# All expert weights in 8 KB runs, two ring slots a step, and fewer unread products between the down steps

## The chip, the cores and the metric

The kernel runs on one core of a Trainium2 chip. The metric is the device time of one execution in microseconds (us), lower is better; three runs of the kernel before gave 1293.96, 1295.03 and 1295.28, median 1295.03. The core has five engines that work side by side and meet at semaphores: TensorE (PE, matrix products; its weight loads are listed as PEld), VectorE (DVE), ScalarE (ACT), GpSimd (POOL) and SyncE (SP, which here only issues DMA transfers). 16 DMA engines move data between HBM and the on-chip memory SBUF, whose rows are its 128 partitions. TensorE writes to eight PSUM banks.

## The reference

256 tokens of width 1024 (float32) pass a first block, a state-space mixer and a mixture of experts, and then four mixer layers. The change touches only the mixture of experts, cut here to what is computed:

```python
def hierarchical_moe(hn, w_router_group, w_router_expert, w_gate, w_up, w_down):
    # 4 groups of 8 experts; each token goes to the 2 best experts of its best group
    ...
    def run_block(args):          # xb: tokens of one expert e
        xb, e = args
        return (jax.nn.silu(xb @ w_gate[e]) * (xb @ w_up[e])) @ w_down[e]
    ...
    out = jnp.zeros((n, d), jnp.float32).at[row_token].add(ys.astype(jnp.float32) * row_gate[:, None])
```

`w_gate` and `w_up` are 32 x 1024 x 512 and `w_down` is 32 x 512 x 1024, all float32: 6 MiB an expert, 192 MiB (201.3 MB) in all. Every expert's weights are read once in each execution.

## The kernel before, in words

The program is a chain of stages: the state-space mixer (`ssd`), the router and the mixture of experts (`moe`), and the layers `fox0`, `gla`, `gdn` and `fox1`. Large weights arrive through a ring of four slots of 2 MiB (`ring`, `SLOTS` = 4), filled by SP. A slot is filled by two DMAs of 1 MiB, one for each half; both raise the semaphore `ready[i]` of the slot.

**The expert stage.** Experts are taken four at a time (`QUAD`), in `NQ` = 8 groups. A group has 12 steps (`MOE_STEPS`), each of which uses one slot: eight for the products with gate and up (`STEPS_UP`), in turn gate and up, then four for down. An up step holds, for four experts, 256 rows of the weight matrix: partition p takes rows 2p and 2p+1 of each expert, which lie side by side in HBM, 2 x 512 x 4 bytes = 4 KB (`up_v`, L437, `r=2`). A down step holds 128 rows of 1024 columns, again 4 KB for each partition and expert (`down_v`, L438). So every slot is loaded in runs of 4 KB (`moe_loads`, L456).

TensorE (`pe_quad`, L2530) waits for the slot of a step, multiplies (8 matmuls, each of which the trace counts as 2 instructions: 16 a step; the four experts share the array side by side, 32 columns each), and raises `ring_used`, on which SP waits before it fills a slot again (L551 in the loop over the groups 2 to 7). Between the up and the down steps TensorE gathers the tokens of the next group (`gather`, L2525), transposes the hidden rows (L2553), and waits for ScalarE's copy of them. After the down steps it scatters the result (L2574). Since partition p holds rows 2p and 2p+1, the gathered tokens are picked with stride 2 (`own` in `gather`), and their norm gains `g_ffn` are laid out to match.

`unread(n, b)` (L2138) issues n small bf16 products into a bank whose result nobody reads. `pe_quad` issues 16 of them before each of the last three down steps.

**The first two groups** are loaded early. Besides the four ring slots they use five further buffers (`extra`, L447) in memory that the stage does not need: group 0 has steps 0 to 3 and 9 to 11 in the ring and 4 to 8 in the extra buffers. So nine steps can be loaded before TensorE has used one; step 9 is the first that waits for `ring_used` (`put`, L504, with `released`).

**After the stage** SP loads the first block of `fox0` behind the last down weights (L509); the other blocks wait for `moe_done`. ScalarE and DVE split each weight block into a high and a low part (L673, L1202).

## Time and profile before

| | |
|---|---|
| median of 3 runs | 1295.03 us (1293.96 to 1295.28) |
| profiled execution, its own time | 1292.94 us |
| its span (first to last instruction) | 1291.2 us |
| TensorE clock granted, mean | 0.964 of full |
| PE / DVE / ACT busy | 86% / 50% / 34% |
| HBM read | 312.52 MB |

The span is cut by the page into 40 slices of 32.3 us. One digit is the share of a slice in which an engine was busy, in tenths; the line GB/s is what the DMA engines moved. The difference of 1.74 us between the time and the span lies around the span, and 2.09 us separate the profiled execution from the median. A granted clock of 1.00 is TensorE's level of 2.4 GHz, 0.50 its level of 1.2 GHz.

### The profile page before, as it was taken

What the parts mean: (1) busy time and instruction counts of PE and PEld (TensorE: products, weight loads), DVE (VectorE), ACT (ScalarE), POOL (GpSimd) and SP (SyncE); (2) the same over time, 40 slices, a digit from 0 to 9 for tenths busy, and PEclk for the clock granted to TensorE, in tenths of its full rate; (3) what the DMA queues carried; (4) which work ended last, traced back from release to release, by engine and by line L of the source; (5) the groups of instructions that cost most, each with busy time, mean ns of one, the idle gap of its engine ahead of it and who ended that gap; (6) DMA issues with size and microseconds to landing.
All of it is one profiled execution on the core that took longest, in us unless ns stands there. A gap on an engine that the chain in (4) does not pass through costs nothing.

```text
span 1291.2 us, 19652 instructions
## 1 busy us (share of the span) xinstructions
PE 1106.5 (86%) x8060; PEld 811.6 (63%) x8060; DVE 644.5 (50%) x1265; ACT 439.2 (34%) x691; POOL 8.0 (1%) x35
## 2 busy tenths in 40 slices
PE   8999899897676758585858999999999979899998
PEld 7999767543131314131414789887779869778897
DVE  6787578420101111020104767667567965656685
ACT  5554435100000000000003556536346653255563
POOL 1000000000000000000000000000000000000000
PEclk9999999999898989898989999999999989899999
DMA  8575345999999999999998974254324530056600
GB/s 299 144 260 196 131 157 196 398 409 409 409 409 410 409 410 410 410 409 410 410 410 296 289 223 155 106 196 143 118 94 168 183 79 4 1 130 172 235 19 33
DMA packets 120005, 314.66 MB, mean 244 GB/s; under 512 B 17139, under 2 KB 17386, under 8 KB 119674
## 3 DMA queue, kind: packets, MB, share of 16 engines
q1 hardware_dynamic: 116864, 310.78, 65.9%
q0 software_dynamic: 352, 2.11, 0.4%
q8 instruction: 54, 0.88, 0.3%
q10 hardware_dynamic: 2714, 0.71, 0.3%
q14 instruction: 21, 0.17, 0.0%
HBM read 312.52 MB, written 1.06 MB: 243 GB/s over the span
## 4 chain that ended last, share of the span: by engine, by line
PE 58%; DMA 28%; DVE 8%; ACT 3%; issue 2%; SPq 1%; DVEq 0%; ACTq 0%
DMA ring<-in_w_up 18%; DMA ring<-in_w_down 10%; PE bank L2250 7%; PE bank L2243 7%; PE bank L2247 7%; PE bank L2225 6%; PE bank L2229 6%; PE bank L2232 6%; PE bank L2540 3%; PE bank L2563 2%; DVE w_l L1202 1%; PE bank L2158 1%; DMA ring<-in_w_in 1%; PE bank L2646 1%; ACT w_h L673 1%
## 5 line engine op out<-in xcount | busy, mean ns | idle before, releaser
L1202 DVE TENSOR_TENSOR w_l<-ring,w_h 128x1024 fp32r<-128x1024 f32 x204 | 246.6, 1221 | 90.7 <-ACT w_h L673 89.0
L673 ACT ACTIVATE w_h<-ring 128x1024 fp32r<-128x1024 f32 x204 | 213.6, 1056 | 176.4 <-PE bank L2232 88.7
L2540 PE MATMUL bank<-ring,cm 128*32 128x512 f32 x880 | 137.1, 754 | 101.0 <-DMA ring<-in_w_gate 61.5
L2540 PEld LDWEIGHTS bank<-ring,cm 128*32 128x32 f32 x880 | 27.7, 124 | 208.6 <-issue 78.5
L2243 PE MATMUL bank<-w_h,hnT_h 128*128 128x512 f32 x480 | 135.6, 405 | 5.1 <-DVE cm L1829 1.9
L2250 PE MATMUL bank<-w_l,hnT_h 128*128 128x512 f32 x480 | 129.7, 392 | 5.5 <-DVE w_l L1202 5.5
L2247 PE MATMUL bank<-w_h,hnT_l 128*128 128x512 f32 x480 | 129.7, 392 | 0.0
L1676 DVE SCALAR_TENSOR_TENSOR cm<-cm,bank 128x512 f32<-128x512 f32 x8 | 5.5, 688 | 215.0 <-ACT cm L895 215.0
L2250 PEld LDWEIGHTS bank<-w_l,hnT_h 128*128 128x128 f32 x480 | 89.6, 188 | 27.4 <-DVE w_l L1202 8.5
L2247 PEld LDWEIGHTS bank<-w_h,hnT_l 128*128 128x128 f32 x480 | 90.6, 189 | 20.0 <-DVE hnT_l L1317 0.2
L2243 PEld LDWEIGHTS bank<-w_h,hnT_h 128*128 128x128 f32 x480 | 86.9, 190 | 25.2 <-issue 4.5
L895 ACT ACTIVATE cm<-bank 128x512 f32<-128x512 f32 x8 | 4.8, 597 | 266.1 <-PE bank L2540 266.1
L2225 PE MATMUL bank<-hnT_h,w_h 128*128 128x256 f32 x576 | 84.1, 289 | 0.0
L2229 PE MATMUL bank<-hnT_l,w_h 128*128 128x256 f32 x576 | 80.9, 283 | 0.0
L2232 PE MATMUL bank<-hnT_h,w_l 128*128 128x256 f32 x576 | 80.8, 283 | 0.0
L2225 PEld LDWEIGHTS bank<-hnT_h,w_h 128*128 128x128 f32 x576 | 74.9, 191 | 2.0 <-issue 1.2
L2563 PE MATMUL bank<-ring,cm 128*32 128x512 f32 x496 | 59.6, 598 | 18.7 <-DMA ring<-in_w_down 13.8
L2232 PEld LDWEIGHTS bank<-hnT_h,w_l 128*128 128x128 f32 x576 | 74.3, 192 | 0.0
L2229 PEld LDWEIGHTS bank<-hnT_l,w_h 128*128 128x128 f32 x576 | 74.3, 192 | 0.0
L1686 DVE COPY cm<-bank 128x512 f32<-128x512 f32 x8 | 5.5, 691 | 124.6 <-PE bank L2563 124.6
L2141 PEld LDWEIGHTS bank<-ident 128*128 128x128 bf16 x446 | 43.4, 102 | 28.0 <-issue 20.1
L2141 PE MATMUL bank<-ident 128*128 128x256 bf16 x446 | 57.1, 285 | 1.6 <-POOLq L587 1.6
(442 smaller groups left out, 1354.9 us busy)
## 6 DMA issues: line engine op xcount, KB each, us to landing
ring<-in_w_down SPq DMA_DIRECT2D x62, 1024.0 KB, 15.9
ring<-in_w_gate SPq DMA_DIRECT2D x56, 1024.0 KB, 15.6
ring<-in_w_up SPq DMA_DIRECT2D x54, 1024.0 KB, 15.8
ring<-in_fox_w_in SPq DMA_DIRECT2D x32, 1024.0 KB, 11.3
ring<-in_w_in SPq DMA_DIRECT2D x22, 1024.0 KB, 9.6
ring<-in_gla_w_in SPq DMA_DIRECT2D x12, 1024.0 KB, 6.3
ring<-in_gdn_w_in SPq DMA_DIRECT2D x12, 1024.0 KB, 6.8
ring<-in_w_out SPq DMA_DIRECT2D x8, 1024.0 KB, 6.3
```

Source lines behind the costliest of these rows:

```text
L673: af(part(w_h, u, width), w, ACT.Copy).then_inc(s["high_ready"], 1)
L1202: v.tensor_tensor(part(w_l, u, width), w, part(w_h, u, width).bitcast(F32), ALU.subtract).then_inc(s["low_ready"], 1)
L2141: mm(bank[b][:, 0:2 * P], ident[:].bitcast(BF16)[:, 0:P], ident[:].bitcast(BF16), start=True, stop=True)
L2158: x = mm(out_rows, w[:, k, c], x_part[:, k, :], start=(w is sw_h and x_part is hnT_h and k == 0), stop=(w is sw_l and k == KD - 1))
L2225: mm(dst, wh[:, k, :], xh[:, k, :], start=(k == 0), stop=False)
L2229: mm(dst, wh[:, k, :], xl[:, k, :], start=False, stop=False)
L2232: x = mm(dst, wl[:, k, :], xh[:, k, :], start=False, stop=(k == KD - 1))
L2243: mm(dst, hnT_h[:, k, tt], wh[:, j, :], start=(first and k == ends[0]), stop=False)
L2247: mm(dst, hnT_l[:, k, tt], wh[:, j, :], start=False, stop=False)
L2250: x = mm(dst, hnT_h[:, k, tt], wl[:, j, :], start=False, stop=(last and k == ends[1]))
L2540: x = mm(bank[a][CAP * e:CAP * (e + 1), :], m_xg[:, 2 * b + r, CAP * e:CAP * (e + 1)], expert_of(w, e)[:, r * FF:(r + 1) * FF], start=(b = ...
L2563: x = mm(bank[3 + n][CAP * e:CAP * (e + 1), :], m_ht[:, c * P + CAP * e:c * P + CAP * (e + 1)], expert_of(w, e)[:, n * BLK:(n + 1) * BLK], ...
```

## The change

**Layout.** `up_v` now takes four adjacent rows for a partition (`r=4`) and `down_v` two, so that a run is 8 KB. One DMA of 1 MiB then holds one expert's rows instead of two experts', and a slot holds two experts instead of four. A matrix product of all four experts needs two slots, so TensorE's loop takes steps in pairs: it waits for both slots, does 16 matmuls (32 instructions), and releases the first slot with the last matmul of expert 1 and the second with that of expert 3. Gate and up alternate by pairs. Tokens and gains are picked with stride 4, the hidden rows with stride 2.

**The last group** is written out behind the loop, on SP and on TensorE. Its last two down steps keep the old form: 4 KB runs, one slot each (`last_v`, `last_loads`, `by_chunk`).

**Unread products.** 24 stand between the two down pairs in place of 16 before each of three steps; group 0 has none; the last group has 24 and then 16 before its two single steps. In a group of the loop that is 24 instead of 48.

**Waits.** ScalarE's tanh of the gate bank waits for 6 released slots instead of 7. The code for tokens beyond an expert's capacity (`ov_slot`) takes two ring slots a step as well; it does not run with these inputs.

```diff
+        g_ffn = sb("g_ffn", [P, 2, KD // 2])
         cols = sb("cols", [16, 8])
...
-        up_v = [w.rearrange("(q j) (b p r) f -> q b p j (r f)", j=QUAD, p=P, r=2) for w in (w_gate, w_up)]
-        down_v = w_down.rearrange("(q j) (c p) n -> q c p j n", j=QUAD, p=P)
+        up_v = [w.rearrange("(q j) (b p r) f -> q b p j (r f)", j=QUAD, p=P, r=4) for w in (w_gate, w_up)]
+        down_v = w_down.rearrange("(q j) (c p r) n -> q c p j (r n)", j=QUAD, p=P, r=2)
+        last_v = w_down.rearrange("(q j) (c p) n -> q c p j n", j=QUAD, p=P)
...
         def moe_loads(halves, q, j):
 
             if j < STEPS_UP:
-                return [(halves[h].rearrange("p (e x) -> p e x", e=QUAD // 2),
-                         up_v[j % 2][q, j // 2][:, 2 * h:2 * h + 2, :]) for h in (0, 1)]
-            return [(halves[h].rearrange("p (e f) -> p e f", e=QUAD // 2),
-                     down_v[q, j - STEPS_UP][:, 2 * h:2 * h + 2, :]) for h in (0, 1)]
+                v, first = up_v[(j // 2) % 2][q, j // 4], 2 * (j % 2)
+            else:
+                v, first = down_v[q, (j - STEPS_UP) // 2], 2 * (j % 2)
+            return [(halves[h], v[:, first + h, :]) for h in (0, 1)]
+
+        def last_loads(halves, q, c):
+
+            return [(halves[h].rearrange("p (e f) -> p e f", e=QUAD // 2), last_v[q, c][:, 2 * h:2 * h + 2, :]) for h in (0, 1)]
...
-                    (g_ffn[:], norm_ffn[0].rearrange("(b p r) -> p b r", p=P, r=2))) + tuple(
+                    (g_ffn[:], norm_ffn[0].rearrange("(b p r) -> p b r", p=P, r=4))) + tuple(
...
-                    with sp.Fori(2, NQ) as q:
+                    with sp.Fori(2, NQ - 1) as q:
                         for j in range(MOE_STEPS):
                             i = (n + j) % SLOTS
                             sp.wait_ge(s["ring_used"], q * MOE_STEPS + (j - SLOTS + 1))
                             sp.sem_inc(s["sp_turn"], 1)
                             for dst, src in moe_loads(ring_halves(i), q, j):
                                 sp.dma_start(dst, src).then_inc(ready[i], 16)
+                    q = NQ - 1
+                    for j in range(MOE_STEPS):
+                        i = (n + j) % SLOTS
+                        sp.wait_ge(s["ring_used"], q * MOE_STEPS + (j - SLOTS + 1))
+                        sp.sem_inc(s["sp_turn"], 1)
+                        for dst, src in (moe_loads(ring_halves(i), q, j) if j < MOE_STEPS - 2 else last_loads(ring_halves(i), q, j - STEPS_UP)):
+                            sp.dma_start(dst, src).then_inc(ready[i], 16)
 
...
 
             def act_quad(it, used, base):
-                act.wait_ge(used, base + STEPS_UP - 1)
+                act.wait_ge(used, base + STEPS_UP - 2)
...
                 pe.wait_ge(s["moe_acc"], acc)
                 for k in ks:
                     for t in range(NT):
-                        own = slice(2 * P * (k // 2) + k % 2, 2 * P * (k // 2 + 1), 2)
+                        own = slice(4 * P * (k // 4) + k % 4, 4 * P * (k // 4 + 1), 4)
                         x = mm(b4(5 + k // 4)[:, k % 4, :], hn[:, t, own], m_S[:, t, :],
                                start=(t == 0), stop=(t == NT - 1))
                     if k % 4 == 3:
...
 
-            def pe_quad(q, it, g, wait_slot, release, second_half=None):
+            def pe_quad(q, it, g, wait_slot, release, second_half=None, by_chunk=False):
                 pe.wait_ge(s["moe_h"], it + 1)
-                for j in range(STEPS_UP):
+                for j in range(0, STEPS_UP, 2):
                     if j == STEPS_UP // 2 and second_half is not None:
                         gather(0, 1, second_half)
                     if j % (STEPS_UP // 2) == 0:
                         pe.wait_ge(s["moe_xg"], g * 2 + (1 + 2 * j // STEPS_UP))
-                    w, a, b = wait_slot(q, j), j % 2, j // 2
-                    for r in (0, 1):
+                    w, a, b = wait_slot(q, j) + wait_slot(q, j + 1), (j // 2) % 2, j // 4
+                    for r in range(4):
                         for e in range(QUAD):
-                            x = mm(bank[a][CAP * e:CAP * (e + 1), :], m_xg[:, 2 * b + r, CAP * e:CAP * (e + 1)], expert_of(w, e)[:, r * FF:(r + 1) * FF],
-                                   start=(b == 0 and r == 0), stop=(b == KD // 2 - 1 and r == 1), tile_position=(0, CAP * e))
-                    x.then_inc(release, 1)
+                            x = mm(bank[a][CAP * e:CAP * (e + 1), :], m_xg[:, 4 * b + r, CAP * e:CAP * (e + 1)], w[e][:, r * FF:(r + 1) * FF],
+                                   start=(b == 0 and r == 0), stop=(b == 1 and r == 3), tile_position=(0, CAP * e))
+                            if r == 3 and e % 2:
+                                x.then_inc(release, 1)
                 gather(g + 1, it + 1)
...
                 for c in range(STEPS_DOWN):
-                    x = tr(b4(2)[:, c, :], m_h[:, c * P:(c + 1) * P], ident[:])
+                    own = slice(2 * P * (c // 2) + c % 2, 2 * P * (c // 2 + 1), 2)
+                    if by_chunk and c >= 2:
+                        own = slice(c * P, (c + 1) * P)
+                    x = tr(b4(2)[:, c, :], m_h[:, own], ident[:])
                 x.then_inc(s["moe_ht"], 1)
                 pe.wait_ge(s["moe_htc"], it + 2)
                 pe.wait_ge(s["moe_acc"], it + 1)
-                for c in range(STEPS_DOWN):
-                    if c:
-                        unread(16, 2)
+
+                def down(c, n, e, w):
+
+                    return mm(bank[3 + n][CAP * e:CAP * (e + 1), :], m_ht[:, c * P + CAP * e:c * P + CAP * (e + 1)], w,
+                              start=(c == 0), stop=(c == STEPS_DOWN - 1), tile_position=(0, CAP * e))
+
+                for c2 in range(1 if by_chunk else 2):
+                    if c2 and second_half is None:
+                        unread(24, 2)
+                    w = wait_slot(q, STEPS_UP + 2 * c2) + wait_slot(q, STEPS_UP + 2 * c2 + 1)
+                    for r in (0, 1):
+                        for n in (0, 1):
+                            for e in range(QUAD):
+                                x = down(2 * c2 + r, n, e, w[e][:, r * D + n * BLK:r * D + (n + 1) * BLK])
+                                if r and n and e % 2:
+                                    x.then_inc(release, 1)
+                for c in (2, 3) if by_chunk else ():
+                    unread(24 if c == 2 else 16, 2)
                     w = wait_slot(q, STEPS_UP + c)
                     for n in (0, 1):
                         for e in range(QUAD):
-                            x = mm(bank[3 + n][CAP * e:CAP * (e + 1), :], m_ht[:, c * P + CAP * e:c * P + CAP * (e + 1)],
-                                   expert_of(w, e)[:, n * BLK:(n + 1) * BLK], start=(c == 0), stop=(c == STEPS_DOWN - 1),
-                                   tile_position=(0, CAP * e))
+                            x = down(c, n, e, expert_of(w, e)[:, n * BLK:(n + 1) * BLK])
                     x.then_inc(release, 1)
 
...
-            with pe.Fori(2, NQ) as q:
+            with pe.Fori(2, NQ - 1) as q:
                 pe_quad(q, q, q, ring_slot, s["ring_used"])
+            pe_quad(NQ - 1, NQ - 1, NQ - 1, ring_slot, s["ring_used"], None, True)
```

The three places at which the order of instructions matters, word for word. A line has the source line, the operation, the bank written and the tile read, and in brackets the semaphores that it waits for; `ring` is the slot ring, `slot_ready0` to `3` its semaphores, x7 seven of the same. Line numbers shift by 13 or more in the changed file.

TensorE at the start of group 0, before:

```order
L2540 MATMUL bank0<-ring,cm 32x512 [waits slot_ready3,moe_xg,moe_h]
L2540 MATMUL bank0<-ring,cm 32x512 x7
L2540 MATMUL bank1<-ring,cm 32x512 [waits slot_ready0]
L2540 MATMUL bank1<-ring,cm 32x512 x7
L2540 MATMUL bank0<-ring,cm 32x512 [waits slot_ready1]
L2540 MATMUL bank0<-ring,cm 32x512 x7
L2540 MATMUL bank1<-ring,cm 32x512 [waits slot_ready2]
L2540 MATMUL bank1<-ring,cm 32x512 x7
L2525 MATMUL bank6<-cm,hn 128x128 [waits moe_acc,moe_sel]
```

TensorE at the same place, now:

```order
L2553 MATMUL bank0<-ring,cm 32x512 [waits slot_ready3,slot_ready0,moe_xg,moe_h]
L2553 MATMUL bank0<-ring,cm 32x512 x15
L2553 MATMUL bank1<-ring,cm 32x512 [waits slot_ready2,slot_ready1]
L2553 MATMUL bank1<-ring,cm 32x512 x15
L2538 MATMUL bank6<-cm,hn 128x128 [waits moe_acc,moe_sel]
```

The four steps of 8 matmuls have become two of 16, and each waits for two slots; the first release stands at the 14th matmul of a step instead of the 8th.

TensorE at the end of a group, before (the loop's last down steps):

```order
L2563 MATMUL bank3<-ring,cm 32x512 [waits slot_ready2]
L2563 MATMUL bank3<-ring,cm 32x512 x3
L2563 MATMUL bank4<-ring,cm 32x512 x4
L2141 MATMUL bank2<-ident 128x256 x16
L2563 MATMUL bank3<-ring,cm 32x512 [waits slot_ready3]
L2563 MATMUL bank3<-ring,cm 32x512 x3
L2563 MATMUL bank4<-ring,cm 32x512 x4
L2141 MATMUL bank2<-ident 128x256 x16
L2588 REGISTER_ALU
L2563 MATMUL bank3<-ring,cm 32x512 [waits slot_ready0]
```

TensorE at the end of the last group, now:

```order
L2577 MATMUL bank3<-ring,cm 32x512 [waits slot_ready1,slot_ready2,moe_acc,moe_htc]
L2577 MATMUL bank3<-ring,cm 32x512 x3
L2577 MATMUL bank4<-ring,cm 32x512 x4
L2577 MATMUL bank3<-ring,cm 32x512 x4
L2577 MATMUL bank4<-ring,cm 32x512 x4
L2154 MATMUL bank2<-ident 128x256 x24
L2577 MATMUL bank3<-ring,cm 32x512 [waits slot_ready3]
L2577 MATMUL bank3<-ring,cm 32x512 x3
L2577 MATMUL bank4<-ring,cm 32x512 x4
L2154 MATMUL bank2<-ident 128x256 x16
L2577 MATMUL bank3<-ring,cm 32x512 [waits slot_ready0]
```

The first two down steps have become one pair; the last two stand as they were, with 24 and 16 unread products (L2141, now L2154) ahead of them.

SP's last loads of the stage, before (inside the loop):

```order
L553 DMA ring<-in_w_down 128x2x1024 [waits ring_used]
L553 DMA ring<-in_w_down 128x2x1024
L550 REGISTER_ALU
L547 REGISTER_ALU
L547 COMPARE_AND_BRANCH
```

SP at the same place, now (behind the loop):

```order
L565 DMA ring<-in_w_down 128x2048 [waits ring_used]
L565 DMA ring<-in_w_down 128x2048
L565 DMA ring<-in_w_down 128x2x1024 [waits ring_used]
L565 DMA ring<-in_w_down 128x2x1024
L565 DMA ring<-in_w_down 128x2x1024 [waits ring_used]
L565 DMA ring<-in_w_down 128x2x1024
```

A half of a slot was 128 partitions x 2 runs of 1024 elements (4 KB); it is now one run of 2048 elements (8 KB), except in the last two steps. SP's order of loads and waits is otherwise the same.

## Rows read from the trace of the kernel before

**Rows 1.** The page, section 2: DMA busy tenths and GB/s by slice.
```profile
DMA  8575345999999999999998974254324530056600
GB/s 299 144 260 196 131 157 196 398 409 409 409 409 410 409 410 410 410 409 410 410 410 296 289 223 155 106 196 143 118 94 168 183 79 4 1 130 172 235 19 33
```

**Rows 2.** The chain that ended last, by line, window 400 to 500 us.
```profile
by line: DMA ring<-in_w_up 71.4%; DMA ring<-in_w_down 35.7%; PE bank L2540 7.9%; SPq L553 2.2%; PE bank L2563 2.0%; issue 1.0%; SPq L551 0.1%
```

**Rows 3.** Timeline of PE, one group: start, us, what, idle time before and its cause.
```profile
464.00 3.62 PE L2540 MATMUL bank<-ring,cm 128*32 128x512 f32 x16 [3.21 <-DMA ring<-in_w_gate]
...
489.59 1.92 PE L2540 MATMUL bank<-ring,cm 128*32 128x512 f32 x16 [1.49 <-DMA ring<-in_w_up]
491.45 4.04 PE L2525 MATMUL bank<-cm,hn 128*128 128x128 f32 x32
...
496.82 1.92 PE L2563 MATMUL bank<-ring,cm 128*32 128x512 f32 x16 [0.69 <-ACT cm L899]
498.68 1.92 PE L2141 MATMUL bank<-ident 128*128 128x256 bf16 x16
500.53 1.92 PE L2563 MATMUL bank<-ring,cm 128*32 128x512 f32 x16
```

**Rows 4.** DMA queues in one group, 423 to 484.44 us: packets, MB, share of 16 engines.
```profile
DMA packets 6528, 25.17 MB, mean 410 GB/s; under 512 B 384, under 2 KB 384, under 8 KB 6528
q1 hardware_dynamic: 6528, 25.17, 102.6%
```

**Rows 5.** The software queue at 747 to 754 us, then at 1192 to 1199 us.
```profile
q0 software_dynamic: 144, 1.05, 36.0%
q0 software_dynamic: 144, 1.05, 35.8%
```

**Rows 6.** Timeline of SP around the first release of a slot.
```profile
223.66 0.88 SPq L509 DMA_DIRECT2D ring<-in_w_up  x2
...
228.11 3.06 SPq L543 DMA_DIRECT2D spare<-in_w_down  x2
244.58 4.63 SPq L509 DMA_DIRECT2D ring<-in_w_down  x6
```

**Rows 7.** Timeline of PE, first two products of group 0.
```profile
242.60 7.07 PE L2540 MATMUL bank<-ring,cm 128*32 128x512 f32 x64 [0.90 <-issue]
249.61 2.15 PE L2525 MATMUL bank<-cm,hn 128*128 128x128 f32 x16
```

**Rows 8.** Windows: us, busy by engine, PEclk, DMA share, GB/s; two restarts, one slow step.
```profile
223.00:224.00 1.00, 1.00 (x10) 0.96 (x9) 1.00 (x2) 0.32 (x1) 0.00 (x0) 1.00 0.00 0
224.00:225.00 1.00, 1.00 (x6) 0.83 (x5) 1.00 (x3) 0.52 (x2) 0.00 (x0) 1.00 0.56 66
...
244.00:246.00 2.00, 2.00 (x24) 0.68 (x19) 0.00 (x0) 0.00 (x0) 0.00 (x0) 1.00 1.17 389
246.00:248.00 2.00, 2.00 (x24) 0.79 (x20) 0.00 (x0) 0.00 (x0) 0.00 (x0) 1.00 0.88 309
248.00:250.00 2.00, 2.00 (x19) 0.71 (x12) 0.00 (x0) 0.00 (x0) 0.00 (x0) 1.00 0.96 373
...
474.40:477.70 3.30, 3.30 (x16) 0.58 (x16) 0.00 (x0) 0.00 (x0) 0.00 (x0) 0.50 1.03 412
```

**Rows 9.** Timeline of PE, end of the last group, and ACT behind it.
```profile
691.14 1.92 PE L2141 MATMUL bank<-ident 128*128 128x256 bf16 x16
694.42 1.92 PE L2563 MATMUL bank<-ring,cm 128*32 128x512 f32 x16 [1.36 <-DMA ring<-in_w_down]
697.34 3.70 PE L2574 MATMUL bank<-cm 128*128 128x512 f32 x8 [1.00 <-DVE cm L1686]
...
699.93 2.95 ACT L673 ACTIVATE w_h<-ring 128x1024 fp32r<-128x1024 f32 x3 [2.92 <-DMA ring<-in_fox_w_in]
```

**Rows 10.** DMA queues at 967 to 970 us, where runs are 2 KB.
```profile
DMA packets 612, 1.22 MB, mean 407 GB/s; under 512 B 16, under 2 KB 16, under 8 KB 612
q1 hardware_dynamic: 612, 1.22, 104.6%
```

**Rows 11.** Windows in which 4 KB runs moved more than 410 GB/s.
```profile
230.00:235.00 5.00, 4.73 (x30) 3.95 (x31) 4.41 (x22) 0.00 (x0) 0.00 (x0) 0.70 1.03 420
250.00:252.00 2.00, 1.76 (x15) 1.56 (x14) 0.20 (x1) 0.00 (x0) 0.00 (x0) 1.00 1.03 420
```

More of the change, by code:

```diff
@@ L246, in build @@
         w_gup = sb("w_gup", [16, BLK])
-        g_ffn = sb("g_ffn", [P, KD // 2, 2])
+        g_ffn = sb("g_ffn", [P, 2, KD // 2])
         cols = sb("cols", [16, 8])
@@ L560, in _ @@
                             with sp.Fori(0, NQ) as q:
-                                for j in range(MOE_STEPS):
-                                    for dst, src in moe_loads(ring_halves(0), q, j):
-                                        sp.dma_start(dst, src).then_inc(ov_ready, 16)
-                                    sp.wait_ge(ov_used, (p - 1) * (NQ * MOE_STEPS) + q * MOE_STEPS + (j + 1))
+                                for j in range(0, MOE_STEPS, 2):
+                                    for i in (0, 1):
+                                        for dst, src in moe_loads(ring_halves(i), q, j + i):
+                                            sp.dma_start(dst, src).then_inc(ov_ready, 16)
+                                    sp.wait_ge(ov_used, (p - 1) * (NQ * MOE_STEPS) + q * MOE_STEPS + (j + 2))
                                     sp.sem_inc(s["sp_turn"], 1)
@@ L2602, in ov_slot @@
                     def ov_slot(q, j):
-                        pe.wait_ge(ov_ready, (p - 1) * (32 * NQ * MOE_STEPS) + q * (32 * MOE_STEPS) + 32 * (j + 1))
-                        return ring_halves(0)
+                        pe.wait_ge(ov_ready, (p - 1) * (32 * NQ * MOE_STEPS) + q * (32 * MOE_STEPS) + 64 * (j // 2 + 1))
+                        return ring_halves(j % 2)
                     with pe.Fori(0, NQ) as q:
```

## The prediction

> **What bounds the kernel now.** I read the slices first. From the eighth to the twenty-first the DMA engines move 398 to 410 GB/s without a break, while TensorE is between 50% and 90% busy [rows 1]. That is the expert stage. The chain that ended last says the same: in 100 us of it nearly all is loads of up and down weights (its pieces overlap, so the shares pass 100%) [rows 2]. The timeline of one group shows TensorE at each step waiting for its slot, 1.5 or 3.2 us, and then working 1.9 or 3.6 us [rows 3]. A group of 12 slots (25.17 MB) takes 61.44 us and repeats to the hundredth. So the end of the stage is set by bytes over rate, counted from where the stream last had to wait for TensorE. Work on TensorE inside a group is free so long as slots come back in time.
>
> **The longer runs.** In one group every DMA engine carries 6144 / 16 = 384 packets of 4 KB (and 24 of under 512 B), so one packet every 61.44 / 384 = 160.0 ns. The packets were busy for 102.6% of 16 x 61.44 us = 1008.6 us, or 164 ns each: each overlaps the next by 4 ns [rows 4]. The trace has packets of 8 KB too, 128 in each of two transfers of the software queue: 36.0% of 16 x 7 us is 40.3 us, 315 ns each, and 35.8% gives 313 [rows 5]. That is 14 ns below two packets of 4 KB (328). With the same overlap of 4 ns an 8 KB packet comes every 310 ns. A slot is 256 such packets, 16 an engine: 4.96 us instead of 5.12, 0.16 us less. If the overlap grows with the packet, 310 becomes 160 x 314/164 = 306 (0.22 us a slot); if runs make no difference to a full stream, it is 320 (nothing). I take 310, the value nearest to the rows of 8 KB themselves.
>
> A page of the Trainium skill speaks against this size of gain: DMA: Bandwidth & Descriptors, section "Why small descriptors are slow (HBM only)", gives a packet about 3 cycles beside one for each 32 bytes, and calls concatenation worth it only up to 256 B. By that, an estimate: 8 KB needs 259 cycles instead of 262, 1.1% of 85 x 5.12 us or 5.0 us, and the whole change would bring 2.8 us (1292.2 us). The rows of 4 and 8 KB show a larger step (14 of 328 ns, 4%), so the trace does not agree with that size; it is weighed as a rival below.
>
> **How many slots gain.** There are 96 slots. The nine of the four ring slots and five further buffers (steps 0 to 8 of group 0) don't wait for TensorE's releases, and the stream then stops for TensorE: SP ended issuing at 231.17 and issued step 9 at 244.58 [rows 6]. What the first nine save is therefore lost at this wait. 87 remain, two of them in 4 KB runs: 85 x 0.16 = 13.6 us saved.
>
> **The first release comes later.** TensorE starts group 0 at 242.60 and needs 7.07 us for four steps, 1.77 each [rows 7]. Before, the first slot was released after one step, by 244.52, and SP issued at 244.58 [rows 6]. By then the stream had nearly run dry: the three windows from 244 to 250 us move 389, 309 and 373 GB/s instead of 410, which is 0.8 us of transfer [rows 8]. Now both slots come back after two steps, 242.60 + 3.6 = 246.2, so step 9 is issued 1.7 us later. An issue into an empty queue brings its first bytes about 1 us later (issued 223.66, none before 224, 66 GB/s in the next microsecond) [rows 6, 8]. The restart is bound by the issue before and after, so the cost is the shift, 1.7 us; if the ramp from fully empty costs another 0.8 us, 2.5. The second pair is released by 250, when 4 MiB (9.9 us) are queued again, so there is no second stop.
>
> **Pairs in the steady groups.** The ring holds two pairs. A pair landed must be released before the next has landed, less 1 us until an issue brings bytes: within 9.92 - 1 = 8.9 us. An up pair takes 3.6 us at the high clock. At the low clock (granted 0.50, 1.2 GHz [rows 8]) a step took 3.62 us, after 3.2 us of idling; the next step had the high clock again [rows 3]. Idling before a pair grows to some 6 us, so I expect each up pair to lose one such stretch: 3.6 + 1.7 = 5.3 us. That fits. After the last up pair come the gather, transposes and copies, 5.4 us from 491.45 to 496.82 [rows 3]; 5.3 + 5.4 = 10.7 us, 0.8 us after the first down pair has landed. It is released at 0.8 + 3.6 = 4.4 us: fits. After it 24 unread products take 2.8 us (16 take 1.86, 498.68 to 500.53 [rows 3]), ready before the second down pair. So these pairs cost nothing; what hides them is the stream, and the price once it fails is in the fourth rival.
>
> **The end.** The last single step runs 1.92 us after the last slot landed, then the scatter follows [rows 9]. This piece is as before. But TensorE must be there: from the start of the last group's down pair it needs 3.6 + 2.8 + 1.9 + 1.9 = 10.2 us, and the last slot lands 10.24 us after that pair. It starts the pair 0.8 us late at 5.3 us an up pair, on time at 3.6, 2.7 us late at 7.2. I take 0.5 us, bounds 0 and 2.7. The first block of the next layer is now issued after the down pair, about 6 us ahead of the last landing, so it still queues directly behind it; ScalarE waits for this block until 699.93 as it does now [rows 9], and all later stages shift as a whole.
>
> **At nothing.** Fewer unread products, and none in group 0: TensorE idles there for loads or runs ahead of them. Stride 4 in the gather: 4.04 us at stride 2; twice that would still be within the 8.9 us. The gains `g_ffn` are half as many small packets. The last group written out: straight code in place of one pass of a loop. ScalarE's tanh keeps a full up pair ahead of its use.
>
> **Sum.** 13.6 - 1.7 - 0.5 = 11.4 us off the profiled execution's 1292.94 (its span of 1291.2 and 1.74 around it): 1281.5. The median of the runs lies 2.09 us higher, so the forecast is **1283.6 us**. By the bounds: at 306 ns 85 x 0.22 = 18.7 less 1.7 gives 1278.0; at 310 with 2.5 and 2.7 lost, 1286.6. The forecast's own range is 1279 to 1288.
>
> **Rivals.**
> *Second, a part of the rate* (9%). In a full stream of 2 KB runs a packet comes every 16 x 3 / (612 - 16) us = 80.5 ns, though busy for 1.046 of that, 84 ns [rows 10]. From 2 to 4 KB the stream thus gained 1 ns in 161, while busy time gained 4 ns in 168. If most of the 14 ns is hidden in the same way and 315 ns are reached, 0.08 us a slot remain: 6.8 - 2.2 = 4.6 us, 1290.4 us. The page's estimate of 1292.2 belongs here.
>
> *Third, no gain in rate* (12%). 2 KB runs stream at 407 GB/s and 4 KB runs at 410 [rows 4, 10]: this looks like a limit that run length doesn't touch. The SP queue may also cut a run of 8 KB in two, as all 8 KB packets seen were the software queue's. Against it: 4 KB runs have moved 420 GB/s for 5 us and for 2 us [rows 11], so memory and ports carry more. Then only the two costs stand: 1295.03 + 2.2 = 1297.2 us, up to 1299.
>
> *Fourth, slower: pairs starve the ring* (7%). If TensorE stays at the low clock through the last up pair and the gather, it takes 7.2 + 8.1 + 2.0 = 17.3 us, the down pair starts 7.4 us late and is released 11.0 us after landing, 2.1 past the 8.9. It decides from a release later than 8.9 us on. Seven groups at 2.1 are 15 us, and the end comes 7.4 us late: 13.6 - 1.7 - 15 - 7.4 = -10.5, 1305.5 us. Against it: in all groups the clock was back after one slow step, and stood at full in the gather [rows 3].
>
> **How the numbers follow.** Forecast 72%, the rivals 9, 12 and 7%. No change means within 0.2%, 2.6 us, about what can be told for this kernel. Faster: the forecast and nearly all of the second, 80%. Same: the third, but for its upper end, and what is left of the second, 11%. Slower: the fourth and the end of the third, 9%. The range starts at 1279.5 and reaches over the second rival to 1293; the third and the fourth lie outside.
>
> **What would show it.** The steady groups: 61.44 us should become 59.5 (12 x 4.96), the stream 410 become 423 GB/s, and packets number half. If the group stays at 61.4, the third rival holds; if the stream drops below its rate once in a group, beside the first down pair, the fourth. The first release should bring SP's issue at 246.2 to 246.5 and a window under 200 GB/s near 246. The last down step should start about 11 us earlier than 694.42, at 683, with little or no idling ahead of it, and the stages behind it should keep their lengths. The forecast is wrong if the group takes over 60.3 us or the later stages change by more than a microsecond.

## The result, and the profile after

The changed kernel takes 1302.21 us (median of 5, 1300.99 to 1307.34), the kernel before 1295.03 us: ratio 1.0062, 95% interval 1.0044 to 1.0081. The forecast was 1283.6 us. The change makes the kernel slower, by 7 to 8 us, and the time lies outside the range given. In other comparisons below the kernel before had medians of 1295 to 1298 us, so only ratios are compared.

The page of the changed kernel, slices and packets, answers [rows 1]:

```profile
PEclk9999999898888878797979999999999989999999
DMA  8575345899999999999997974353325530045600
GB/s 298 140 262 195 130 164 196 363 422 420 398 395 424 399 423 397 423 400 422 400 422 252 290 228 140 121 195 130 130 69 185 173 94 3 2 128 168 231 25 33
DMA packets 95687, 314.70 MB, mean 242 GB/s; under 512 B 16883, under 2 KB 17130, under 8 KB 71290
```

The stream now alternates between slices at 420 GB/s or more and slices at about 400, where every slice was 409 or 410. The rate is there, and something takes it away again. One group of 61.3 us, 409.5 to 470.83 us, as in [rows 4]:

```profile
GB/s 411 422 417 422 422 411 427 422 427 411 427 427 427 422 427 422 427 411 411 427 411 427 422 417 427 144 198 427 417 427 427 427 427 427 427 427 427 417 427 422
q1 hardware_dynamic: 3454, 25.15, 99.0%
```

Each slice is 1.53 us. 38 of the 40 run at 411 to 427 GB/s, two at 144 and 198: there is one stop a group. TensorE's timeline around it (start, duration, idle time before), which answers [rows 3]:

```profile
429.38 6.20 PE L2553 MATMUL bank<-ring,cm 128*32 128x512 f32 x32 [3.84 <-DMA ring<-in_w_up]
435.51 7.73 PE L2538 MATMUL bank<-cm,hn 128*128 128x128 f32 x32
...
444.63 3.64 PE L2577 MATMUL bank<-ring,cm 128*32 128x512 f32 x32 [0.69 <-ACT cm L912]
448.20 2.79 PE L2154 MATMUL bank<-ident 128*128 128x256 bf16 x24
```

The last up pair takes 6.20 us and the gather 7.73, in place of 4.04. So the first down pair, which landed some 9.9 us after 429.38, isn't started before 444.63 nor released before 448.2. SP's issues (SPq is SP's queue; x8 are four slots in two halves each), and the stream there (windows: length, PE busy, granted clock, DMA share, GB/s):

```profile
425.68 11.91 SPq L558 DMA_DIRECT2D ring<-in_w_down  x8
448.50 2.19 SPq L558 DMA_DIRECT2D ring<-in_w_gate  x4
```
```profile
430.00:434.00 4.00, 4.00 (x24) 0.50 1.00 418
436.00:442.00 6.00, 6.00 (x28) 1.00 1.01 422
448.00:449.00 1.00, 1.00 (x12) 1.00 0.30 123
449.00:450.00 1.00, 1.00 (x12) 1.00 0.68 90
450.00:451.00 1.00, 1.00 (x14) 1.00 0.69 262
451.00:452.00 1.00, 1.00 (x12) 1.00 1.03 434
```

In the three windows from 448 us 475 of 3 x 422 = 1266 are moved, a loss of 791 / 422 = 1.9 us. A group of 12 slots at 4.96 us is 59.5 us, and 59.5 + 1.9 = 61.4, the old period.

There are six such stops, near 325, 387, 449, 511, 571 and 633 us. At the first two the last up pair had taken only 5.34 us. The second, with TensorE, SP and the stream:

```profile
368.86 5.34 PE L2553 MATMUL bank<-ring,cm 128*32 128x512 f32 x32 [4.51 <-DMA ring<-in_w_up]
...
383.24 3.64 PE L2577 MATMUL bank<-ring,cm 128*32 128x512 f32 x32 [0.69 <-ACT cm L912]
```
```profile
387.12 2.17 SPq L558 DMA_DIRECT2D ring<-in_w_gate  x4
```
```profile
386.00:387.00 1.00, 1.00 (x14) 1.00 0.73 303
387.00:388.00 1.00, 1.00 (x11) 1.00 0.14 57
388.00:389.00 1.00, 1.00 (x11) 1.00 1.04 164
389.00:390.00 1.00, 1.00 (x11) 1.00 0.79 336
```

The loss is again 828 / 422 = 2.0 us, and this group takes 61.42 us (399.64 - 338.22). The two ends of the stage, as in [rows 6, 7, 9]:

```profile
248.66 4.33 SPq L514 DMA_DIRECT2D ring<-in_w_down  x6
```
```profile
240.10 4.00 PE L2538 MATMUL bank<-cm,hn 128*128 128x128 f32 x16 [0.70 <-DVE cm L1664]
245.00 7.07 PE L2553 MATMUL bank<-ring,cm 128*32 128x512 f32 x64 [0.90 <-issue]
...
676.41 5.34 PE L2553 MATMUL bank<-ring,cm 128*32 128x512 f32 x32 [4.60 <-DMA ring<-in_w_up]
...
690.77 3.64 PE L2577 MATMUL bank<-ring,cm 128*32 128x512 f32 x32 [0.69 <-ACT cm L912]
...
700.78 1.92 PE L2577 MATMUL bank<-ring,cm 128*32 128x512 f32 x16
703.72 3.67 PE L2604 MATMUL bank<-cm 128*128 128x512 f32 x8 [1.02 <-DVE cm L1699]
```

Step 9 is issued at 248.66 in place of 244.58 (+4.1 us), and the scatter starts at 703.72 in place of 697.34 (+6.4). A low-clock stretch in a later stage adds most of another 1.7 us; the span is 1299.3 us, 8.1 longer. At its start (both kernels wait 2.2 us for VectorE before it, but the old one's four products take 1.20 us):

```profile
898.30 1.68 PE L2263 MATMUL bank<-w_l,hnT_h 128*128 128x512 f32 x4 [2.22 <-DVE w_l L1215]
899.77 1.91 PE L2256 MATMUL bank<-w_h,hnT_h 128*128 128x512 f32 x4
```

### The profile page after: what moved, and what is told of

The parts are those of the page before. It is cut to its first block, busy times and chain, and to the rows that moved or that the text cites. A ratio compares the mean times of both kernels' runs of the same rounds, so it can differ in the third digit from the quotient of the medians.

```text
span 1299.3 us, 19222 instructions
## 1 busy us (share of the span) xinstructions
PE 1122.6 (86%) x7860; PEld 839.6 (65%) x7860; DVE 644.7 (50%) x1265; ACT 439.6 (34%) x691; POOL 8.1 (1%) x35
## 4 chain that ended last, share of the span: by engine, by line
PE 70%; DMA 16%; DVE 8%; ACT 3%; issue 2%; SPq 1%; ACTq 0%; DVEq 0%
DMA ring<-in_w_up 15%; PE bank L2263 7%; PE bank L2256 7%; PE bank L2553 7%; PE bank L2260 7%; PE bank L2242 6%; PE bank L2238 6%; PE bank L2245 6%; PE bank L2538 5%; PE bank L2577 4%; PE bank L2154 2%; DVE w_l L1215 1%; SPq L558 1%; PE bank L2171 1%; DMA ring<-in_w_in 1%
## 5 line engine op out<-in xcount | busy, mean ns | idle before, releaser
L2553 PE MATMUL bank<-ring,cm 128*32 128x512 f32 x880 | 144.7, 809 | 103.5 <-DMA ring<-in_w_up 66.7
L2553 PEld LDWEIGHTS bank<-ring,cm 128*32 128x32 f32 x880 | 37.3, 142 | 209.2 <-issue 150.1
L2538 PEld LDWEIGHTS bank<-cm,hn 128*128 128x128 f32 x288 | 68.0, 329 | 8.6 <-issue 7.8
L2538 PE MATMUL bank<-cm,hn 128*128 128x128 f32 x288 | 69.9, 402 | 0.7 <-DVE cm L1664 0.7
L2577 PE MATMUL bank<-ring,cm 128*32 128x512 f32 x496 | 58.2, 595 | 4.8 <-ACT cm L912 4.8
```

The source lines that it names most:

```text
L2538: x = mm(b4(5 + k // 4)[:, k % 4, :], hn[:, t, own], m_S[:, t, :], start=(t == 0), stop=(t == NT - 1))
L2553: x = mm(bank[a][CAP * e:CAP * (e + 1), :], m_xg[:, 4 * b + r, CAP * e:CAP * (e + 1)], w[e][:, r * FF:(r + 1) * FF], start=(b == 0 and r = ...
L2577: return mm(bank[3 + n][CAP * e:CAP * (e + 1), :], m_ht[:, c * P + CAP * e:c * P + CAP * (e + 1)], w, start=(c == 0), stop=(c == STEPS_DOW ...
```

## The experiments

Twelve kernels were run, in four comparisons with the kernel before. The table keeps start and stream apart: when step 9 is issued, how long it is from there to the transposes behind the stage ("stage"; 701.98 - 244.58 = 457.4 us in the kernel before), and the stream over 270 to 670 us, all from profiled executions. Between the scatter and these transposes run 5 waits 1.1 us longer than the others and run 8 0.5 us longer, outside the stream; where that matters the scatter is used instead.

| kernel | step 9 | stage | GB/s | ratio, 95% interval |
|---|---|---|---|---|
| before | 244.58 | 457.4 | 409 | |
| changed | 248.66 | 459.7 | 410 | 1.0062 [1.0044, 1.0081] |
| 1 changed, packed gather | 247.51 | 453.2 | 413 | 0.9969 [0.9939, 0.9999] |
| 2 before, stride 4 | 247.25 | 458.3 | 409 | 1.0038 [1.0013, 1.0063] |
| 3 changed, 4 KB runs | 250.23 | 467.6 | 403 | 1.0115 [1.0081, 1.0148] |
| 4 before, packed gather | 244.72 | 457.5 | 409 | 0.9989 [0.9966, 1.0012] |
| 5 = 1 + 40 unread products | 246.88 | 446.9 | 421 | 0.9964 [0.9942, 0.9986] |
| 6 changed + 40 unread | 250.66 | 449.5 | 419 | 0.9984 [0.9963, 1.0005] |
| 7 = 5 + halved first pair | 245.41 | 446.0 | 421 | 0.9941 [0.9922, 0.9961] |
| 8 = 5 in 4 KB runs | 252.12 | 459.8 | 409 | 1.0054 [1.0032, 1.0076] |
| 9 = 7, 8 KB to the end | 248.54 | 448.3 | 421 | 0.9955 [0.9938, 0.9971] |
| 10 = 7 with 24 unread | 249.52 | 445.9 | 421 | 0.9952 [0.9926, 0.9977] |
| 11 = 7 without unread | 245.19 | 454.6 | 413 | 0.9959 [0.9934, 0.9983] |
| 12 = 7 with 32 unread | 245.70 | 446.6 | 421 | 0.9928 [0.9900, 0.9956] |

**1. The gather without a stride.** VectorE writes the normalised tokens already in the order in which the gather reads them.

```
-  v.tensor_scalar(hn[:, t, :], x_res[:, t, :], ...
+  v.tensor_scalar(hn[:, t, :].rearrange("p (b r j) -> p b r j", r=4, j=P),
+                  x_res[:, t, :].rearrange("p (b j r) -> p b r j", r=4, j=P), ...
-  own = slice(4 * P * (k // 4) + k % 4, 4 * P * (k // 4 + 1), 4)
+  own = slice(P * k, P * (k + 1))
```

> The changed kernel, but the normalized tokens are stored permuted (VectorE writes them so), and the gather reads its 128 columns side by side. Theory S (the stride of 4 doubles the gather, 7.73 us instead of 4.04, and that lets the stream of weights stop once in each group): gather at most 4.0 us, no stop, 59.5 us a group, last scatter about 18 us earlier than in the changed kernel (703.7), median about 1284 us. Rival P (working in pairs of slots is itself too coarse for a ring of four slots): gather shorter, but the stop in each group stays, median over 1296. Rival C (the low clock of TensorE in the up pairs, with fewer unread products): up pairs still take 6 us and a stop of about 1 us a group remains, median about 1291.

The gather takes 3.84 us, and the ratio falls from 1.0062 to 0.9969, 12 us, give or take 5; by the trace the scatter comes 7.6 us earlier (696.08 for 703.72). The stride was most of what was wrong. But 1284 us and a scatter 18 us earlier were expected, and the stream makes only 413 GB/s: up pairs are still slow, and some dips remain. That is rival C (1291 us) and not theory S alone (timeline and two windows of this kernel):

```profile
425.68 6.26 PE L2554 MATMUL bank<-ring,cm 128*32 128x512 f32 x32 [3.77 <-DMA ring<-in_w_up]
431.88 3.84 PE L2539 MATMUL bank<-cm,hn 128*128 128x128 f32 x32
...
437.10 3.64 PE L2578 MATMUL bank<-ring,cm 128*32 128x512 f32 x32 [0.69 <-ACT cm L912]
```
```profile
434.00:435.00 1.00, 1.00 (x12) 1.00 1.02 270
435.00:436.00 1.00, 1.00 (x11) 1.00 0.72 303
```

**2. The stride alone, in the kernel before.** The gather reads every fourth column instead of every second; it gathers other columns, so only the time counts.

```
-  own = slice(2 * P * (k // 2) + k % 2, 2 * P * (k // 2 + 1), 2)
+  own = slice(4 * P * (k // 4) + k % 4, 4 * P * (k // 4 + 1), 4)
```

> The kernel before, with the gather reading tokens with stride 4 instead of 2 (it gathers other columns than the weights in the slots belong to: only the time counts). Theory S: gather 7.7 us in each group; with one slot a step the ring absorbs it (the first down step starts 3.7 us later, its slot is due 15 us after that), so the groups stay at 61.44 us; only the first release (2 us) and the end of the last group (about 2 us) are later: median about 1299. Rival P: the stride costs little by itself, under 1 us: 1295 to 1296.

The gather takes 7.73 us, the groups keep 61.44 us (from 404.62 to 466.06), step 9 comes 2.7 us later and the stage is 0.9 us longer. With single slots, back in time, the stride costs only the start and the tail: 3.6 us by the trace, 5 us (2 to 8) in the median, where 4 were expected.

**3. The changed kernel in runs of 4 KB**, with its pairs and strides. A slot holds half the run of all four experts.

```
-  return [(halves[h], v[:, first + h, :]) for h in (0, 1)]
+  own = slice((j % 2) * (SLOT // QUAD), (j % 2 + 1) * (SLOT // QUAD))
+  return [(halves[h]..., v[:, 2 * h:2 * h + 2, own]) for h in (0, 1)]
```

> The changed kernel with the same pairs, strides and unread products, but every slot loaded in 4 KB runs (a slot holds half of the run of all four experts). Theory S: a slot takes 5.12 us again and the stream does not stop, since the down pair is released 18.9 us after the last up pair landed and the deadline moves from 18.8 to 19.5 us; 61.44 us a group, the same as with 8 KB, so a median within 3 us of the changed kernel, 1300 to 1305. If instead the faster stream still gives most of its gain, this is 8 us or more slower than the changed kernel, 1310.

The stage is 8 us longer than the changed kernel's and the stream at 403 GB/s, under the old 409. So the changed kernel had kept a part of its faster stream. The guess of 1300 to 1305 us was a miss: stops cost the slower stream too. The ratio of 1.0115 stands for 1310 us, the other value named.

**4. The packed gather in the kernel before**, by the edit of run 1 with r=2.

> The kernel before, with the tokens stored permuted so that the gather reads side by side instead of with stride 2. Theory S: the weight load of the gather falls from 196 ns to about 120 to 190 ns, the gather from 4.04 us to 3.9 or less; groups stay at 61.44, the start of group 0 moves by less than 0.5 us either way (VectorE's permuted write may cost 0.7 us): no change within 1 us of 1295.

No change, 0.9989. Packing by itself brings nothing there, so what it brought in run 1 is the cure of the stride.

**5. The clock of the up pairs.** In `pe_quad`, ahead of the waits for the second to fourth up pair:

```
+  if j and second_half is None:
+      unread(40, 2)
```

> The kernel with the packed gather, and 40 unread products (about 4.65 us at 24 in 2.79) ahead of the waits for the second, third and fourth up pair of every group but the first. Theory C (what is left after the packed gather is the low clock: TensorE idles 6.3 us before an up pair, then works at 1.2 GHz for 6.0 to 6.2 us of the pair, so that the first down pair is released too late once a group): the up pairs take 3.64 us, the dip to about 300 GB/s beside the first down pair goes, a group takes 59.5 us in place of 60.9 to 61.4, seven groups bring 6 to 9 us, and the time comes to 1283 to 1287, ratio 0.991 to 0.993 against the kernel before. Rival M (the memory or the queue gives no more than 413 GB/s over a group, and the dips are its own): the pairs get short, the group stays at 60.9 or more, the time stays at 1291 to 1293 (0.997).

The dips are gone, the up pairs of the steady groups take 3.64 us, and a group takes 59.7 us (first gate pairs at 394.88 and 454.58 us). Timeline, and two windows of 60 us:

```profile
404.74 3.64 PE L2556 MATMUL bank<-ring,cm 128*32 128x512 f32 x32 [1.74 <-DMA ring<-in_w_up]
...
414.77 3.64 PE L2556 MATMUL bank<-ring,cm 128*32 128x512 f32 x32 [1.92 <-DMA ring<-in_w_gate]
```
```profile
300.00:360.00 60.00, 46.42 (x387) 1.00 1.01 421
420.00:480.00 60.00, 46.45 (x387) 1.00 1.01 422
```

By the trace the stage is 6.3 us shorter than in run 1, and 7.4 us if it is taken to the scatter (441.2 for 448.6). The median doesn't show it: 0.9964 after 0.9969, from different comparisons, where 0.991 to 0.993 were expected. In the profiled execution the stages behind the transposes took 595.8 us, in that of the kernel before 589.2: see "Later stages" and runs 11 and 12.

**6. The same products with the stride left in.**

> The changed kernel (gather with stride 4, 7.7 us) with the same 40 unread products ahead of the up pairs. By the deadline sum: from the landing of the last up pair 3.64 + 7.73 + about 1.3 (transposes, copies) = 12.7 us until TensorE starts the first down pair, 2.8 after its landing; released at 6.4 us, within 8.9. So if stride and low clock only matter through the sum of both, this kernel streams at 59.5 us a group as well and lands within 2 to 3 us of the kernel with both cures (1286 to 1289: group 0 still starts 1.2 us later and its gather is 2 us longer). Rival: the slow gather costs by itself (weight loads from the same memory as the landing packets, or a chain ScalarE and VectorE that hangs on it), then the group stays above 60.5 and the time near 1296 to 1300.

From 420 us on the stream makes 422 GB/s with the gather of 7.73 us still there; TensorE releases the first down pair 6.4 us after its landing. So the stride fits as long as the pairs are quick: it needs the low clock beside it to stop the groups, while the low clock alone still costs some (run 1). What the stride costs by itself is the start (step 9 at 250.66, where the clock was low as well), a stop before 360 us (408 GB/s from 300 to 360) and a small one behind it (419 from 360 to 420).

```profile
430.52 3.64 PE L2555 MATMUL bank<-ring,cm 128*32 128x512 f32 x32 [1.75 <-DMA ring<-in_w_up]
434.10 7.73 PE L2538 MATMUL bank<-cm,hn 128*128 128x128 f32 x32
...
443.21 3.64 PE L2579 MATMUL bank<-ring,cm 128*32 128x512 f32 x32 [0.69 <-ACT cm L912]
```
```profile
420.00:480.00 60.00, 50.04 (x382) 1.00 1.01 422
```

**7. An early first release.** Steps 0 and 1 of group 0 in half runs of all four experts, released one after the other:

```
+  if j < 2 and isinstance(q, int) and q == 0:     # in moe_loads: 4 KB runs, as in run 3
-  if r == 3 and e % 2:
+  if (r % 2 and e == 3) if halved else (r == 3 and e % 2):
       x.then_inc(release, 1)
```

> The kernel with the packed gather and the 40 unread products, and also the first gate pair of group 0 in runs of 4 KB that hold half a run of all four experts, so that its first slot is released after one step (8 products a half, 1.8 us) as in the kernel before. If the start is as the prediction took it (the shift of the first release is lost one for one), step 9 is issued 1.7 us earlier, and the end comes 1.7 us earlier than in the kernel without it: 1282 to 1285, ratio about 0.990. Rival: the stream restarts from a deeper empty queue or stops a second time for the next pair, the gain is then under 0.8 us.

Step 9 is issued 2.0 us after TensorE's first product at 243.43, where run 5 needs 3.7 us (243.22 to 246.88): the 1.7 us of the prediction. The scatter comes 1.2 us earlier (686.84 for 688.05), or 1.4 us counted from that first product. The transposes come 2.3 us earlier, but 1.1 of these are a wait that only run 5's execution has. The ratio is 0.9941, where about 0.990 was expected.

**8. Everything cured, in 4 KB runs.**

> The kernel with the packed gather and the 40 unread products, but all its expert weights in runs of 4 KB (a slot holds half a run of all four experts; the same pairs, waits and strides). With no stop left in the stream, this differs from the kernel in 8 KB runs by the rate alone. By the prediction's term (0.16 us a slot, 85 slots) it is 13.6 us slower: 1297 to 1300, with groups of 61.4 us against 59.5. Rival: run length gives nothing to a stream that doesn't stop, then both take the same time and the same group.

```profile
420.00:480.00 60.00, 49.80 (x374) 0.91 1.03 410
```

409 GB/s against 421, the stage 459.8 us against 446.9: 12.9 us, and 13.5 us to the scatter (454.7 against 441.2). The ratios differ by 0.0090, or 11.7 us, give or take 4. Its profiled execution also started group 0 at the low clock.

**9. Pairs to the end.** The last two steps as a pair of 8 KB runs, like the others.

```
-  (moe_loads(...) if j < MOE_STEPS - 2 else last_loads(ring_halves(i), q, j - STEPS_UP))
+  moe_loads(ring_halves(i), q, j)
-  pe_quad(NQ - 1, NQ - 1, NQ - 1, ring_slot, s["ring_used"], None, True)
+  pe_quad(NQ - 1, NQ - 1, NQ - 1, ring_slot, s["ring_used"])
```

> The best kernel so far (packed gather, 40 unread products before the up pairs, first gate pair of group 0 in half runs; it measured 0.9941), but with the last two steps of the last group in runs of 8 KB as well, so that its last work is a pair. Read of the single steps: after the last landing 1.92 us of products and the scatter. With a pair it is 3.64 us: the scatter comes 1.7 us later after the landing, less 0.2 to 0.3 us for the faster last slots, so 1.3 to 1.7 us slower, ratio 0.995 to 0.9955. Rival: the last single steps start late there anyway (TensorE needs 10.2 us from the first down pair to the scatter), then the pair costs nothing or under 0.5 us.

From TensorE's start on the last weights to the scatter it takes 686.29 to 692.24, 5.95 us, where run 7 takes 2.94 (683.90 to 686.84): 3 us, 1.7 of them the pair and 1.3 the low clock after 3.64 us of idling. The stage grows by 2.3 us, the ratio by 0.0014, less than the intervals tell apart.

```profile
686.29 4.92 PE L2585 MATMUL bank<-ring,cm 128*32 128x512 f32 x32 [3.64 <-DMA ring<-in_w_down]
692.24 3.67 PE L2612 MATMUL bank<-cm 128*128 128x512 f32 x8 [1.04 <-DVE cm L1703]
```

**10. 24 unread products in place of 40.**

> The best kernel so far with 24 unread products (2.79 us) ahead of an up pair in place of 40 (4.54 us), so that TensorE idles about 3.5 us before each up pair in place of 1.7. Before the second down pair the same 24 with 3.5 us of idling left the pair at 3.64 us. If that holds for up pairs too, the groups stay at 59.7 us and the time at 0.993 to 0.995. Rival: the clock falls again in some pairs (5.3 to 6.2 us); since with the packed gather the first down pair is then still released near the deadline, some groups show a dip and the time is 2 to 4 us longer. It also asks whether TensorE's extra work in the expert stage is what makes single low-clock stretches in later stages more frequent: if so there are fewer here.

Of the 18 up pairs behind unread products (337 to 673 us) ten take 3.64 us, five 5.1 to 5.3, and three (at 357.79, 487.35 and 606.71 us) 6.2 to 6.4; the stream makes 421 GB/s. So pairs released up to 5.3 us after landing cost nothing, and of the three slow ones between quick ones two not either; beside the first (364 to 366 us) the stream falls to 377 GB/s, 0.2 us.

**11 and 12. Run 7 with none, and with 32.**

> The best kernel so far without any unread products ahead of the up pairs: packed gather and halved first pair alone. It asks for the low clock's own price in the median, since the trace gave 6.3 us of the expert stage to the unread products (groups of 60.9 to 61.4 against 59.7) while the ratios of the two kernels were 0.9969 and 0.9964. If the trace is typical: 4 to 7 us slower than the kernel with 32 of them in this same comparison, ratio 0.997 to 1.000. Rival (the profiled execution had bad luck with the clock, most runs have no dips, or the unread products cost later what they save): within 2 us of it.

> The best kernel so far with 32 unread products (about 3.65 us) ahead of an up pair, between the 40 and the 24 already run, in one comparison with the kernel without any. Up pairs 3.64 us, 421 GB/s over the steady groups, group of 59.7 us, ratio 0.992 to 0.996. Rival as above: no better than the kernel without them.

Medians 1292.68 and 1287.29 us in one comparison on one chip, 5.4 us apart. The two ratios share their runs of the kernel before, so their intervals overstate the uncertainty; set directly against each other, run 12 is the faster in 64 of the 72 pairs of one execution of each. The trace says the same: 413 against 421 GB/s, the stage 454.6 against 446.6 us. Of the 18 up pairs behind unread products in run 12 five take 5.1 to 5.3 us in place of the expected 3.64, and the rate holds even so. The execution profiled without them was among that kernel's slowest (1299.03 of 1286.04 to 1299.06 us), so 8 us is more than the typical price. In it (windows):

```profile
414.00:416.00 2.00, 0.00 (x0) 1.00 0.66 209
436.00:438.00 2.00, 2.00 (x20) 1.00 0.78 246
```

The first of the two dips follows an up pair of 6.49 us that was ready at 407.19 and came back at 413.7. Two thirds of the next pair had been moved by then, and the stream falls though that pair has not landed. The trace marks when each of the 16 DMA engines ends its part of a transfer: the second half of the slot that landed at 417.09 had its first mark at 414.39, 2.7 us earlier. A slot counts as landed with its slowest engine; the others had nothing left by then but what SP had issued at 413.84, and its first bytes come about 1 us after the issue. The marks lie 1.2 to 1.3 us apart at the two pairs of 6.3 us in run 10 that cost nothing, and 1.9 us at the one that cost 0.2. This fits, but no run varied that spread by itself.

Run 12 (0.9928) and run 7 (0.9941) beat both kernels; their intervals overlap.

## Why the prediction was wrong

**Packets of 8 KB: right.** 310 ns a packet was to bring 423 GB/s and 59.5 us a group. Undisturbed windows show 422 to 424 GB/s, an undisturbed group takes 59.7 us (311 ns a packet), and runs 5 and 8 put 12.9 us on it (13.5 to the scatter) where the term said 13.6. The second rival's 315 ns are out by this. The step of 3% from 409 to 421 GB/s also decides against the 1.1% that I had worked out from the Trainium skill (DMA: Bandwidth & Descriptors, "Why small descriptors are slow (HBM only)"), and against the third rival.

**The failed step: the deadline "9.92 - 1 = 8.9 us", and with it the stride of 4 "at nothing" ("twice that would still be within the 8.9 us").** The gather did take nearly twice 4.04 us. With my own 5.3 us for the up pair the sum was 0.8 + 4.0 + 3.6 = 8.4 us from landing to release, inside the deadline. The changed kernel has this very case: in the group of the up pair at 368.86 that pair takes 5.34 us, the down pair landed at 378.8 and came back at 386.9, 8.1 us later, and the stream stopped for 2.0 us. Where the up pair took 6.20 us the release came 9.0 us after landing (6.20 + 7.73 + 1.3 + 3.64 - 9.92), by the deadline 0.1 us late, and 1.9 us were lost. So the low clock beyond my 5.3 us added nothing here; the 8.9 us were wrong. Run 6 releases 6.4 us after landing and loses nothing that counts.

Two things make the deadline shorter. I had taken 1 us from an issue to its first bytes, but the full rate comes later. In the kernel before, after the issue at 223.66 and the 66 GB/s of [rows 8], the trace goes on with

```profile
225.00:226.00 1.00, 1.00 (x7) 1.00 0.92 246
226.00:227.00 1.00, 1.00 (x9) 1.00 0.82 319
```

so up to 228 us (373 GB/s in the last microsecond) 1.9 us of transfer are missing, not 1. And a slot counts as landed with its slowest engine: the marks of the last slot before the stop lie 0.5 us apart at 449 us, 2.1 us at 389. An estimate: release less loss, 9.0 - 1.9 and 8.1 - 2.0, puts the last release without loss 6 to 7 us after landing. Runs 1 and 6 then show what made the release late, one by one: without the stride 413 GB/s and 12 us gained, with the stride but quick pairs 422 GB/s and 10 us gained. What fewer unread products cost is nothing that shows: the down pairs around them took 3.64 us in every group.

**The fourth rival (7%, 1305.5 us) was the one that came.** Its sign, a drop once in a group beside the first down pair, is what the trace shows. Its clock story was half right: the last up pair is at the low clock for about 5 of its 6.2 us (granted 0.50 from 430 to 434), but the gather ran at the full clock (1.00) and was slow by its stride. That its 1305.5 us come near 1302.2 is partly luck: it has seven stops of 2.1 us and 7.4 us for the end, where the trace has six of 1.9 and 4.4, and it has 1.7 for the start, which took 4.1. What I held against it, that one slow step brings the clock back, came from steps of 16 products after 3.2 us of idling; after 3.8 to 6.2 us the low clock held for 3 to 5 us of a pair (a pair of 5.34 us has lost 1.7, one of 6.20 us 2.6, at half the full rate).

**First release: 1.7 us taken, 4.1 measured.** The 1.7 is right for the pair (run 7 takes it away again). The other 2.4 us are TensorE's later start, 245.00 for 242.60: the first half of the gather stands before it and takes 4.00 us for 2.15, and it began 0.55 us later (240.10 for 239.55), which no run explains. I had looked for the stride's cost only where the stream hides it. Run 2 has the same shift, 2.7 us.

**Tail: 0.5 taken, bounds 0 and 2.7, 4.4 measured.** The last up pair landed at 676.4, so the down pair behind it by 686.3, and TensorE starts it at 690.77, 4.4 us late. From there it needs 13.0 us to the scatter and waits for no slot. Both bounds had the gather at 4.04 us; with 5.34 + 7.73 + 1.3 us the start must come 4.4 us late.

**Sum.** Start +4.1, tail +4.4, later stages +1.7, together 10.2 us; the span grew by 8.1, so the groups brought 2.1. That agrees with 13.6 us less six stops of 1.9. Run 5, which is the changed kernel with both cures, has its scatter 9.3 us earlier than the old one, where the forecast said 11.4; so the sum was near for a kernel that gives its slots back in time. Run 12, which also has run 7's early release, ends the expert stage 9.7 us earlier.

**Later stages.** They shift as a whole, but not always at the old length: from the transposes behind the expert stage to those at about 1176 us it takes 474.4 us before, 476.2 in the changed kernel, 474.4 in run 12 and 482.8 in run 11. Stretches at the low clock after short waits make the difference. More work on TensorE before isn't needed for them, since run 11, without it, has as much as any. What decides which execution gets them is open; they can hide in a median what the stage gains, as in run 5.

## What to carry to other kernels

Where slots come back in larger bundles, write the time from landing to release as one sum with each term at its worst row. Compare it with a deadline that is read from a restart up to its full rate, not to its first bytes (here 6 to 7 us and not 8.9). An operand that TensorE loads with a stride of 4 float32 can cost much more than one with a stride of 2, also where it stands ahead of the first release: let the engine that writes the operand put it in order. Here TensorE, after waiting 3.8 to 6.2 us for a pair, did most of that pair at the lower clock, so a larger gap between bundles can lengthen the bundle.

## What the runs showed of the hardware

Weight loads of 128 x 128 float32 follow the stride of what they read. Median ns over the steady groups, with stride 2 (before), 4 (changed) and packed (run 1):

```profile
L2525 PEld LDWEIGHTS bank<-cm,hn x224: 192/196/197, 307.2 to 679.4; 128*128 128x128 f32 x112
```
```profile
L2538 PEld LDWEIGHTS bank<-cm,hn x192: 307/329/332, 312.5 to 627.0; 128*128 128x128 f32 x192
```
```profile
L2539 PEld LDWEIGHTS bank<-cm,hn x212: 186/192/192, 312.3 to 680.0; 128*128 128x128 f32 x106
```

Stride 2 is nearly free, stride 4 costs two thirds more. The time at stride 4 was the same at both clocks: the first 16 products took 4.00 us at a granted 0.51 to 0.64 (240.10 us) and 4.00 at full clock (252.00), while the packed ones took 3.78 us at the low clock and 2.05 at the full (run 8). On VectorE, the permuted write of 128 x 1024 took 1142 ns with r=4 (run 1) for 750 unpermuted, and 751 with r=2 (run 4).
